# Modulations of a two-layer conditioned block, computed in rounds of 2048 columns and spread over four stages

## The reference, cut to what matters

```python
c_act, cc_act = jax.nn.silu(c), jax.nn.silu(c_ctx)
for l in range(2):
    mod  = c_act  @ w_mod[l] + b_mod[l]          # (1, 6144), w_mod[l] is 1024 x 6144
    modc = cc_act @ w_mod[l] + b_mod[l]
    sh1, sc1, g1, sh2, sc2, g2 = split(mod, 6)   # the same for modc
    px = (rmsnorm(x, norm1_g[l]) * (1 + sc1) + sh1) @ w_in[l] + b_in[l]
    x  = x + g1 * (mix(px) @ w_out[l])
    x  = x + g2 * swiglu(rmsnorm(x, norm2_g[l]) * (1 + sc2) + sh2, w_gu[l], w_down[l])
```

## Time and profile before

| | |
|---|---|
| median of three runs | 2475.97 us |
| the profiled execution: span | 2476.8 us; the profile gives no time outside it |
| `fox`: modulation turns on PE | 120.6 to 193.8 us |
| `ret`: modulation turns on PE | 948.0 to 1013.4 us |
| first mixer of x, its first projection product | 1708.57 us |
| PE, VectorE (DVE), ScalarE (ACT) busy | 89%, 45%, 36% of the span |

### The profile page before, as it was taken

One profiled execution on the slowest core, in us unless ns is written; L12 is line 12 of the kernel. 1 busy time (PEld: TensorE's weight loads), 2 busy tenths in 40 slices (PEclk: granted clock), 3 DMA queues, 4 the chain that ended last, 5 costly groups with the idle time before them and its releaser, 6 DMA issues. The chain is left out here.

```text
span 2476.8 us, 45087 instructions
## 1 busy us (share of the span) xinstructions
PE 2212.2 (89%) x19490; PEld 1781.4 (72%) x19490; DVE 1124.2 (45%) x1982; ACT 886.7 (36%) x1491; POOL 70.8 (3%) x94
## 2 busy tenths in 40 slices
PE   7998798897686999879999998877888998898999
PEld 7867466664463997767777775644778998777999
DVE  5355335433432643553333333423755555746554
ACT  5434232133211552332222223323444444444443
POOL 0000000000000000000000000000000000000001
PEclk9999899999898999989999999888888999988999
DMA  7494999999999567759999999898313555413551
GB/s 263 154 346 155 372 413 400 379 398 406 391 400 363 187 197 273 270 214 357 405 409 407 397 416 416 332 375 298 136 35 124 183 179 156 151 35 110 181 178 61
DMA packets 254384, 676.27 MB, mean 273 GB/s; under 512 B 12640, under 2 KB 65888, under 8 KB 254176
## 3 DMA queue, kind: packets, MB, share of 16 engines
q1 hardware_dynamic: 238848, 614.77, 65.8%
q0 software_dynamic: 15328, 58.50, 6.1%
HBM read 672.17 MB, written 1.05 MB: 272 GB/s over the span
## 5 line engine op out<-in xcount | busy, mean ns | idle before, releaser
L448 PE MATMUL bank<-xx,high 128*128 128x256 f32 (+1 forms) x3296 | 632.1, 293 | 35.0 <-DVE xx L587 22.5
L448 PEld LDWEIGHTS bank<-xx,high 128*128 128x128 f32 (+1 forms) x3296 | 522.6, 194 | 90.3 <-issue 60.9
L448 PE MATMUL bank<-xx,low 128*128 128x256 f32 (+1 forms) x1648 | 474.2, 288 | 0.0
L448 PEld LDWEIGHTS bank<-xx,low 128*128 128x128 f32 (+1 forms) x1648 | 320.5, 194 | 1.4
L397 DVE TENSOR_TENSOR low<-lane,high 128x1024 fp32r<-128x1024 f32 (+1 forms) x112 | 130.7, 1170 | 310.2 <-ACT high L386 310.2
L386 ACT ACTIVATE high<-lane 128x1024 fp32r<-128x1024 f32 (+1 forms) x112 | 113.1, 1014 | 292.3 <-PE bank L448 292.3
L448 PE MATMUL bank<-hx,high 128*128 128x256 f32 x1056 | 197.1, 288 | 0.0
L448 PEld LDWEIGHTS bank<-hx,high 128*128 128x128 f32 x1056 | 164.1, 191 | 16.1 <-issue 15.2
L448 PE MATMUL bank<-hx,low 128*128 128x256 f32 x528 | 149.0, 282 | 0.0
L1400 ACT ACTIVATE hs<-bank 64x256 f32<-64x256 f32 x64 | 24.1, 377 | 290.0 <-PE bank L1387 289.9
L1407 DVE TENSOR_TENSOR hs<-hs,bank 64x256 f32<-64x256 f32 x64 | 27.1, 423 | 209.2 <-ACT hs L1400 208.8
(11 more groups left out here) (556 smaller groups left out, 4082.7 us busy)
## 6 DMA issues: line engine op xcount, KB each, us to landing
ring__15<-in_expert_w_gu SPq DMA_DIRECT2D x52, 1024.0 KB, 10.3
ring__14<-in_expert_w_gu SPq DMA_DIRECT2D x51, 1024.0 KB, 10.3
ring__16<-in_expert_w_gu SPq DMA_DIRECT2D x51, 1024.0 KB, 10.2
ring__50<-in_expert_w_gu SPq DMA_DIRECT2D x26, 1024.0 KB, 10.4
ring__16<-in_expert_w_down SPq DMA_DIRECT2D x26, 1024.0 KB, 8.8
ring__14<-in_expert_w_down SPq DMA_DIRECT2D x26, 1024.0 KB, 9.1
ring__146<-in_expert_w_gu SPq DMA_DIRECT2D x26, 1024.0 KB, 9.6
ring__49<-in_expert_w_gu SPq DMA_DIRECT2D x25, 1024.0 KB, 11.1
```

The source lines that it names most:

```text
L448: done = pe.matmul(out, a.bitcast(F32R), b.bitcast(F32R), start=it["start"] and k == 0 and q == 0 and not halves, stop=stop)
```

## The change

A round is now 2048 columns, three to a layer, and a round is eight units. A unit is one load of 128 rows x 2048 columns (a row of it is 8 KB) and four products, in which each column tile holds other columns: tile `j` holds columns `512 j` to `512 j + 511` of the round, and the eight units add up in one bank, which is held from the first unit to the last. ACT then copies it once, PE turns it by four products of 8 output columns, and DVE adds `b_mod` to 16 column groups at once and makes the gain that the round completes (`gm_v` has a key for each of the two gains).

The 48 units are spread: `fox` does 16 (rounds 0 and 1 of layer 0), `ret` 16 (round 2 of layer 0, round 0 of layer 1), the first mixer of `x` 12 (round 1 of layer 1 and half of round 2), the feed-forward part after it 4. In `fox` and `ret` step `i` does the units from `ceil(16 i/12)` to `ceil(16 (i+1)/12)`, two or one. In the mixer eight units stand between the column sums and the projection, and four after the first two items of the output projection; in the feed-forward part four stand ahead of the projections. Their loads stand among those of the projections in SP's order. The activations `silu(c)` are made once, in `fox` by ACT, and copied by POOL into each stage's `cs`.

```diff
-        mods = space(ctx, "mods", 256)
+        mods, c_silu = space(ctx, "mods", 256), space(ctx, "c_silu", KC, 2)
...
         class Modulation:
 
+            def __init__(self, name, room, rounds, first=0, row=None):
+                self.name, self.room = name, room
+                self.units = [(L, r, k) for L, r in rounds for k in range(KC)][first:]
+                self.cs = room("cs", KC, 32)
+                self.rows = Turns([room("mod_row", 512) if row is None else row], kept)
+
+            def ends(self, i):
+
+                return [self.units[u][:2] for u in self.at(i) if self.units[u][2] == KC - 1] if i >= 0 else []
+
+            def at(self, i):
+
+                n = len(self.units)
+                return range(min(n, -(-n * i // 12)), min(n, -(-n * (i + 1) // 12)))
+
+            def sp(self, sp, units):
+                for L, r, k in units:
+                    ring.load(sp, ("mod", L, r, k), self.room, A["w_mod_2"][L, k * P:(k + 1) * P, SLOT * r:SLOT * (r + 1)], 1, SLOT)
+
...
+            def silu_act(self, act):
+                act.activation(c_silu[:, :, 0], V("cc"), ACT.Silu)
+                act.activation(c_silu[:, :, 1], V("c"), ACT.Silu).then_inc(*mod_row.up("silu"))
+
+            def setup_pool(self, pool):
+                pool.memset(self.cs, 0.0).then_inc(*mod_set.up((self.name, "zero")))
+                pool.wait_ge(*mod_set.at((self.name, "zero")))
+                pool.wait_ge(*mod_row.at("silu"))
+                pool.tensor_scalar(self.cs[:, :, 0:2], c_silu, 1.0, None, MUL).then_inc(*mod_set.up(self.name))
+
+            def unit_pe(self, pe, unit):
+                L, r, k = unit
+                key = ("mod", L, r)
+                pe.wait_ge(*mod_set.at(self.name))
+                if k == 0:
                     banks.next(key)
+                    banks.hold(key)
+                    for s, q in banks.freed(key):
+                        pe.wait_ge(*s.at(q))
+                w = ring.view(self.room, ("mod", L, r, k), 4, 512)
+                pe.wait_ge(*ring.ready(("mod", L, r, k)))
+                for j in range(4):
+                    n = pe.matmul(banks[key][32 * j:32 * j + 32, :], self.cs[:, k, :], w[:, j, :], start=k == 0, stop=k == KC - 1,
+                                  tile_position=(0, 32 * j))
+                n.then_inc(*mod_mm.up((L, r, k)))
+                ring.free(("mod", L, r, k), (mod_mm, (L, r, k)))
+                if k == KC - 1:
+                    banks.release(key)
...
+            def row_act(self, act, L, r):
+                row = self.rows.next((L, r))
+                act.wait_ge(*mod_mm.at((L, r, KC - 1)))
+                for s, q in self.rows.freed((L, r)):
+                    act.wait_ge(*s.at(q))
+                act.activation(row, banks[("mod", L, r)][:, :], ACT.Copy).then_inc(*mod_row.up((L, r)))
+                banks.free(("mod", L, r), (mod_row, (L, r)))
...
+            def turn_pe(self, pe, L, r):
+                key, row = ("turn", L, r), self.rows[(L, r)]
+                banks.next(key)
+                for s, q in banks.freed(key):
+                    pe.wait_ge(*s.at(q))
+                pe.wait_ge(*mod_row.at((L, r)))
+                used = ident.rearrange("p (a b) -> p a b", a=4)[:, :, 0:2]
+                for j in range(4):
+                    n = pe.matmul(banks[key][:, 8 * j:8 * j + 8], row[:, j * P:(j + 1) * P], used, start=True, stop=True)
+                n.then_inc(*mod_turn.up((L, r)))
+                self.rows.free((L, r), (mod_turn, (L, r)))
...
+            def out_dve(self, dve, L, r):
+                key = ("turn", L, r)
+                mod = mods[:, 128 * L:128 * L + 96].rearrange("p (c v) -> p c v", v=2)
+                gm = mods[:, 128 * L + 96:128 * L + 128].rearrange("p (i c v) -> p i c v", i=2, c=8)
+                dve.wait_ge(*mod_turn.at((L, r)))
+                dve.tensor_tensor(mod[:, 16 * r:16 * r + 16, :].rearrange("p (j c) v -> p j c v", j=4),
+                                  banks[key][:, 0:32].rearrange("p (c j v) -> p j c v", c=4, j=4),
+                                  bc(V("b_mod", 48 * L + 16 * r, 16).rearrange("p (j c) -> p j c", j=4), [P, 4, 4, 2], 3), ADD).then_inc(
+                    *mod_out.up((L, r)))
+                banks.free(key, (mod_out, (L, r)))
+                if r == 1:
...
                     return
+                i, nm, sc = ((0, "norm1", 8), None, (1, "norm2", 32))[r]
+                dve.wait_ge(*mod_out.at((L, r)))
+                dve.scalar_tensor_tensor(gm[:, i], mod[:, sc:sc + 8, :], 1.0, bc(V(nm, 8 * L, 8), [P, 8, 2], 2), ADD, MUL).then_inc(
+                    *gm_v.up((L, i)))
+
+            def step_pe(self, pe, i):
+                for u in self.at(i):
+                    self.unit_pe(pe, self.units[u])
+                for L, r in self.ends(i - 1):
+                    self.turn_pe(pe, L, r)
+
+            def step_act(self, act, i):
+                for L, r in self.ends(i):
+                    self.row_act(act, L, r)
+
+            def step_dve(self, dve, i):
+                for L, r in self.ends(i - 1):
+                    self.out_dve(dve, L, r)
...
-            mod = Modulation(0, room)
+            mod = Modulation("fox", room, [(0, 0), (0, 1)])
...
                 proj.loads(sp, 4, len(proj.items))
-                for i in range(12):
-                    mod.sp(sp, i)
+                mod.sp(sp, mod.units)
                 outp.sp(sp)
...
                         *wf_in.up(q0, 16))
+                mod.setup_pool(pool)
...
                         values_pe(pe, i - 2)
-                    if i < 13:
-                        mod.pe(pe, i)
+                    mod.step_pe(pe, i)
                 out_proj_pe(pe, outp, early)
...
-                mod.setup_act(act)
+                mod.silu_act(act)
...
-                    if i < 13:
-                        mod.act(act, i)
+                    mod.step_act(act, i)
...
                 events_wait(dve, in_done)
-                mod.setup_dve(dve)
...
-                    if i < 13:
-                        mod.dve(dve, i)
+                    mod.step_dve(dve, i)
                 out_low(dve, range(2, KC))
-                mod.gains_dve(dve)
...
-            mod = Modulation(1, room)
+            mod = Modulation("ret", room, [(0, 2), (1, 0)])
...
-                for i in range(12):
-                    mod.sp(sp, i)
+                mod.sp(sp, mod.units)
...
                 pool.dma_start(tab, A["ret_tab"]).then_inc(*tab_in.up("tab", 16))
+                mod.setup_pool(pool)
...
-                schedule(scores, values, centre, var, lambda i: mod.pe(pe, i))
+                schedule(scores, values, centre, var, lambda i: mod.step_pe(pe, i))
...
-                mod.setup_act(act)
-                schedule(lambda h: None, values, centre, var, lambda i: mod.act(act, i))
+                schedule(lambda h: None, values, centre, var, lambda i: mod.step_act(act, i))
...
-                mod.setup_dve(dve)
-                schedule(scores, lambda h: None, centre, var, lambda i: mod.dve(dve, i))
-                mod.gains_dve(dve)
+                schedule(scores, lambda h: None, centre, var, lambda i: mod.step_dve(dve, i))
...
+            mod = Modulation(name, get, [(1, 1), (1, 2)], row=ut.rearrange("p a t -> p (a t)")) if v and not L else None
...
             def loads(e):
+                if mod:
+                    mod.sp(e, mod.units[0:1])
+                    proj.loads(e, 0, 2)
+                    mod.sp(e, mod.units[1:2])
+                    proj.loads(e, 2, 4)
+                    mod.sp(e, mod.units[2:8])
+                    proj.loads(e, 4, len(proj.items))
+                    outp.loads(e, 0, 4)
+                    mod.sp(e, mod.units[8:12])
+                    outp.loads(e, 4, len(outp.items))
+                    return
                 proj.sp(e)
                 if not states_only:
...
                 if v and not L:
                     norm.weights(pool)
+                if mod:
+                    mod.setup_pool(pool)
...
             def pe(pe):
                 norm.sums(pe)
+                if mod:
+                    for unit in mod.units[0:8]:
+                        mod.unit_pe(pe, unit)
...
                         continue
                     at = it["at"]
+                    if mod and at == ends["gate"] + 4:
+                        mod.turn_pe(pe, 1, 1)
...
                     next(turns)
                     next(turns)
+                if mod:
+                    for unit in mod.units[8:12]:
+                        mod.unit_pe(pe, unit)
...
                         gate_rows_act(act)
+                        if mod:
+                            mod.row_act(act, 1, 1)
                     if at == ends["gate"] + 3:
...
-                dve.wait_ge(*gm_v.at(L))
+                dve.wait_ge(*gm_v.at((L, 0)))
+                if not states_only:
+                    dve.wait_ge(*mod_out.at((L, 1)))
...
                         continue
```

(83 more changed lines are left out.)

19 lines of the change are left out of this document (removed).

## The result

The changed kernel takes 2493.8 us (median of 15 runs, 2482.4 to 2506.9), the kernel before 2478.1 in the runs beside it. The ratio is 1.0068, 95% interval 1.0052 to 1.0084: slower by 0.7%, some 16 us, where 13 us less were forecast.

A forecast was written before the change was run, and what follows sets the result against it. PE was taken to bound fox and ret until the DVE and ACT chain limits, with PE and DMA full at the mixer's start. Fox -15.3, ret -8.2, mixer +6.5, +1.0, +1.8, feed-forward +1.0 gave -13.2: 2462.8 us, range 2450 to 2475.

The forecast's parts named there:

- The step that failed: Between fox and the first expert stage: fox's saving is not swallowed, so all later work shifts as a whole.
- Sum: Whole kernel: -15.3 - 8.2 + 6.5 + 1.0 + 1.8 + 1.0 = -13.2 us, giving 2462.8 us.
- Fox, -15.3: Step loop of fox: fewer loads and turnings shorten steps to a mean of 4.3 us; -15.3 us (-12 to -17.5).
- The bank held: Fox: a held bank leaves 7 of 8; costs 0, or about 0.4 us where an eviction is late.
- Ret, -8.2: Heads of ret: last root 11.2 us earlier, less 1.0 clock charge for each of three heads; -8.2 us (-5 to -11).
- the case against the change: Ret: with values and `var` at 1.2 GHz in every head, the 1.0 us charge would be up to 4.7.
- Mixer, +9.3 with its tail and turning: First mixer of x: late units and lower clock at the start +6.5 us, turning +1.0, four tail units +1.8.
- The price of the tail's four units: Mixer's tail: four units of 3.7 us ahead of the transposes, half hidden; +1.8 us (0 to +4).
- a slower HBM side: Mixer's start: by the skill page's 358 GB/s, against 386 in the trace, the third late unit comes 0.7 us later.
- Feed-forward, +1.0: Feed-forward part: four units fit into PE's 5.04 us wait for the norm; the turning in a full stretch costs +1.0 us.
- Rival C, slow 8 KB rows: Loads in all changed stages: each unit occupies DMA for 5.1 us, one after another; +12 us, 2488 us; chance 0.10.

The follow-up runs named there:

- the change with its slots in place: Changed kernel with c_silu laid into unused bytes of the buffer spare, so ring slots begin at the earlier kernel's multiples of 512 bytes: 2463.9 us, ratio 0.9937.
- a_pad192: Changed kernel with 192 unused bytes added behind c_silu, so slots begin 256 bytes past a multiple of 512: 2459.8 us, ratio 0.9932 to the kernel before.
- n_best: n_rec with round 2 of layer 0 moved from ret into fox (24 units in fox, 8 in ret): 2467.2 us, ratio 0.9962 to the kernel before.
- n_ret24: Changed kernel with c_silu in spare, round 1 of layer 1 moved from the mixer's start into ret (24 units there): 2468.9 us, ratio 0.9958.
- n_two: Changed kernel with c_silu in spare, all 48 units in fox and ret, none in mixer or feed-forward part: 2476.0 us, ratio 0.9979.
- n_rec: Changed kernel with c_silu in spare, the eight units at the mixer's start moved into its recurrence, two per step: 2461.5 us, ratio 0.9953.

## Why the prediction was wrong

**The step that failed** is the one in its first paragraph: what leaves `fox` early "is not swallowed by the stage behind", since DMA waits before the first `moe`, "so all later work shifts as a whole". The time was not swallowed, but the later work did not only shift: its loads land 64 bytes off and take longer. The term was not in the sum at all, and it is +30 us (2493.8 against 2463.9). I went through the diff for instructions and left out its one line of memory. The Trainium skill, "DMA: Bandwidth & Descriptors", section How a descriptor splits into AXI transactions, has the rule that I did not weigh: a descriptor is split into transactions that must start at 256-byte boundaries, so one that starts off a boundary can take a transaction more. The page speaks of what is read; here it is the address written that moved. These runs agree with its boundary (64 and 128 off cost, 256 does not). For a 4 KB row of an expert matrix the page would make it 17 pieces for 16, an estimate of 6%; no run here counts pieces, and what was measured is 3% in the rate of a full DMA, 1.2% and 12% in the time of the two queues, and 5% to 23% in the landing times above. Why q0 lost so much more than q1 stays open.

The other steps, held against the change with its slots in place:

- **Sum.** -13.2 was forecast, to 2462.8. Measured were 2463.9 and 2459.8. The forecast of the change proper was right, in part by luck: by the stages of the kernel with its slots in place `fox` gave 11.7 for 15.3, which the other terms made good (mixer +8.1 for +9.3, feed-forward nothing for +1.0, `ret` -9.1 for -8.2).
- **Fox, -15.3.** Its loop took 91.1 us before, 76.8 to 78.1 in four kernels with 16 units: -13 to -14.3. Of this the stage kept 11.7, because the loop began 2.6 us later in that execution; its start lies between 118.4 and 121.0 in kernels whose instructions are those of before. The timeline of PE in the changed kernel, the lines that answer to the steps of the earlier trace rows:

```profile
154.72 0.70 PE L963 MATMUL bank<-kt,qt 64*128 64x256 f32 x2 [1.21 <-ACT mod_row L807]
...
164.50 0.70 PE L963 MATMUL bank<-kt,qt 64*128 64x256 f32 x2
...
168.45 0.70 PE L963 MATMUL bank<-kt,qt 64*128 64x256 f32 x2
...
171.48 1.06 PE L795 MATMUL bank<-ring__18,cs 128*32 128x512 f32 x8
172.36 1.04 PE L795 MATMUL bank<-ring__19,cs 128*32 128x512 f32 x8
173.34 0.70 PE L963 MATMUL bank<-kt,qt 64*128 64x256 f32 x2
```

  A step with one unit is 3.95 us (164.50 to 168.45; forecast 4.1), with two 4.89 (forecast 4.76), the mean 4.26 (forecast 4.3), and a unit 0.88 (171.48 to 172.36). The bank held, put at 0 or 0.4, costs 1.21 in the first line: scores ask for the bank that still waits for its row's copy. The changed kernel's own loop took 81.1, 3 us more than its siblings, and the clock shows where. From 130 to 150 us, in the steps of the first heads, it was granted 0.50 and then 0.76, and a_pad192, with the same instructions, 0.63 and then 1.00 (granted clock, DMA share, GB/s at the end of a line), the changed kernel first:

```profile
130.00:140.00 10.00, 10.00 (x45) 7.44 (x44) 4.72 (x13) 3.08 (x13) 0.00 (x0) 0.50 0.52 163
140.00:150.00 10.00, 10.00 (x57) 5.43 (x56) 5.70 (x15) 3.41 (x14) 0.00 (x0) 0.76 0.57 210
```

```profile
130.00:140.00 10.00, 10.00 (x55) 7.32 (x53) 5.70 (x16) 2.86 (x12) 0.00 (x0) 0.63 0.51 161
140.00:150.00 10.00, 9.90 (x71) 5.22 (x69) 7.91 (x17) 4.40 (x17) 0.00 (x0) 1.00 0.91 344
```

  The two are level at 129.3 us and 3.3 us apart at the first wait for a row's copy (154.72 and 151.42). In both the lower clock began behind PE's wait of 1.56 us for DVE at 127 us. The prediction charged the clock in `ret` and in the mixer, not in `fox`. That the shift has a part in it is not shown: by itself it did not lengthen the loop (89.6 against 91.1).
- **Ret, -8.2.** The stage lost 7.8 in the changed kernel, 9.1 without the shift. ACT's roots, which answer to the earlier trace rows:

```profile
955.10 0.47 ACT L2001 ACTIVATE rs<-bank,vec 128x256 f32<-128x256 f32 x1
...
967.98 0.47 ACT L2001 ACTIVATE rs<-bank,vec 128x256 f32<-128x256 f32 x1 [1.13 <-PE bank L1958]
...
981.59 0.47 ACT L2001 ACTIVATE rs<-bank,vec 128x256 f32<-128x256 f32 x1 [1.13 <-PE bank L1958]
...
995.17 0.47 ACT L2001 ACTIVATE rs<-bank,vec 128x256 f32<-128x256 f32 x1 [3.59 <-PE bank L1958]
```

  The roots are 12.9, 13.6 and 13.6 us apart, where 13 to 14 was named. The lower clock through values and `var` in every head, which was the case against the change, did not come (it came in n_best, where the units were too few to fill PE's waits). In the kernel without the shift it is seen in the last head, where `var` takes 3.63 us behind a gap, for 1.89 elsewhere:

```profile
976.94 3.63 PE L1959 MATMUL bank<-tmp,vec 128*128 128x256 f32 x8 [4.45 <-ACT tmp L1997]
```
- **Mixer, +9.3 with its tail and turning.** +9.0 in the changed kernel, +8.1 without the shift and +5.8 with a_pad192. The price of the tail's four units, put at 1.8, can't be told from nothing: the mixer took 168.8 us in n_ret24, which has only them, 169.5 in n_two, which has none, and 165.9 to 169.0 in the kernels with the instructions of before. At its start PE waited as worked out, for the units whose slots came late:

```profile
1716.42 1.07 PE L795 MATMUL bank<-ring__16,cs 128*32 128x512 f32 x8
...
1721.24 1.06 PE L795 MATMUL bank<-ring__207,cs 128*32 128x512 f32 x8 [1.19 <-DMA ring__207<-in_w_mod]
1723.74 1.06 PE L795 MATMUL bank<-ring__16,cs 128*32 128x512 f32 x8 [1.43 <-DMA ring__16<-in_w_mod]
1726.22 1.06 PE L795 MATMUL bank<-ring__17,cs 128*32 128x512 f32 x8 [1.42 <-DMA ring__17<-in_w_mod]
1728.74 1.93 PE L795 MATMUL bank<-ring__206,cs 128*32 128x512 f32 x8 [1.45 <-DMA ring__206<-in_w_mod]
1730.60 0.61 PE L448 MATMUL bank<-xx,high 128*16 128x256 f32 x2
```

  The late units stand 2.5 us apart, where 2.7 was taken from the distance of loads of this matrix. The eight units end 14.2 us after the sums (1716.4 to 1730.6), where 12.6 was worked out. The prediction's 0.7 us for a slower HBM side is too high by its own numbers: three distances of 2.9 for 2.7 us are 0.6, and nothing hangs on it.
- **Feed-forward, +1.0.** -1.2 from there to the end: the units were hidden, and so was the turning. In n_two, which has neither there, it is 606.7 us, for 607.1 with them. Where the 1.2 us come from no run shows.
- **Rival C, slow 8 KB rows**, ended near the measured time (2488) for another reason. Its mechanism is refuted: loads at 2.5 us, no step of `fox` that ends in a wait for DMA, and 2463.9 with the same rows. It gave the side of slower a chance of 0.10; the mechanism that did it had none.

## What to carry to other kernels

A diff is also read for what it allocates. Where a stage is bound by DMA, note the address at which its transfers land, before and after, and keep small lasting buffers behind the large ones or in an unused corner of another. When a stage whose code is the same takes longer, compare a queue that carries the same packets and bytes in both kernels: its share of the span tells slower transfers from more transfers. And before work is taken out of a loop whose engines wait for each other, ask what its absence does to the clock of PE: in n_best eight units fewer saved nothing.

## What the runs showed of the hardware

- Loads of 1 MB into 128 partitions are slower when they land 64 or 128 bytes past a multiple of 256 in the partition (ratios 1.0132, 1.0138 and 1.0130), and not at 256 past a multiple of 512 (1.0003). The same 58.50 MB of GpSimd's queue took 6.8% of the span for 6.1%. A DMA that was never idle moved 392 to 393 GB/s for 402 to 406. Expert loads landed after 10.8 us for 10.3. Other offsets, and smaller transfers alone, were not tried.
- PE fell to the lower clock behind waits of 3.3 and 3.5 us for DVE (two products of 128x128 in 0.63 us for 0.39, granted clock 0.77 and 0.89, n_best), and kept 1.00 where eight units more stood in those waits (n_rec).
- Work on PE is not hidden by the gaps of PE in a chain of several engines: 8 units, 7 us, cost 12 us in `ret` on top of sixteen, where they waited for their own loads, and nothing on top of eight; about 7 at the mixer's start with their turning, as much in its recurrence, and 1 to 3 in `fox`.
